# Gated delta rule recurrence: block-inverse joins as 32x32 and 64x64 products in tiles of the TensorE array

## The reference, cut to what matters

```python
lmat = jnp.where(strict, beta[..., :, None] * kk * decay, 0.0)
a = lmat + jnp.eye(CHUNK, dtype=lmat.dtype)
rhs = jnp.concatenate([v * beta[..., None], k * (beta * jnp.exp(g))[..., None]], axis=-1)
sol = lax.linalg.triangular_solve(a, rhs, left_side=True, lower=True, unit_diagonal=True)
...
def step(S, inp):
    v_new = u_c - jnp.einsum("bhcd,bhde->bhce", w_c, S)
    o_c = (jnp.einsum("bhcd,bhde->bhce", qd_c, S)
           + jnp.einsum("bhij,bhje->bhie", qk_c, v_new))
    S = S * gl_c[..., None, None] + jnp.einsum("bhcd,bhce->bhde", kd_c, v_new)
    return S, o_c
```

## Time and profile before

| what | value |
|---|---|
| time, median of 3 executions | 1723.73 us (1723.07 to 1731.12) |
| time of the profiled execution | 1730.97 us |
| its span on the core | 1729.2 us |
| PE busy | 1676.2 us, 97% of the span, 9103 matmul records |
| DVE, ACT, POOL busy | 49%, 40%, 50% |
| the recurrence | from 233.7 us to 507.1 us of the span |
| mean granted TensorE clock | 0.991 of full speed |

### The profile page before, as it was taken

The page is one execution under the profiler, slowest core; times in us unless marked ns, Lnnn a source line. Parts: engine busy times, 40 slices in busy tenths (PEclk is TensorE's granted clock), DMA queues, the critical chain, the costliest instruction groups (busy, mean ns, idle before and its releaser), DMA issues.

```text
span 1729.2 us, 22778 instructions
## 1 busy us (share of the span) xinstructions
PE 1676.2 (97%) x9103; PEld 1448.7 (84%) x9103; DVE 850.3 (49%) x1343; ACT 685.3 (40%) x1010; POOL 865.8 (50%) x485
## 2 busy tenths in 40 slices
PE   7999899999999999999999999999999999999997
PEld 7898889999989888888888887888887778888886
DVE  7778956824334201222111112127999974357754
ACT  5655444233232222234222223334233354366651
POOL 4455434233335544544555555446467466356661
PEclk9999899999999999999999999999999999999999
DMA  5476179454322324322322333333222322223332
GB/s 204 143 247 178 62 215 281 119 166 149 121 74 86 98 97 146 98 89 95 98 97 98 97 96 101 100 108 93 94 96 84 110 86 87 97 98 98 101 104 75
DMA packets 121264, 202.41 MB, mean 117 GB/s; under 512 B 32560, under 2 KB 71624, under 8 KB 121160
## 3 DMA queue, kind: packets, MB, share of 16 engines
q1 hardware_dynamic: 119400, 197.98, 36.1%
q10 hardware_dynamic: 1760, 2.98, 0.5%
HBM read 170.97 MB, written 29.97 MB: 116 GB/s over the span
## 4 chain that ended last, share of the span: by engine, by line
PE 80%; DVE 14%; ACT 2%; issue 2%; DMA 1%; SPq 0%; POOL 0%; DVEq 0%; ACTq 0%
PE ps L421 66%; DVE ps L1268 4%; PE ps L1775 4%; DVE cacc L2231 3%; PE ps L897 1%; PE ps L950 1%; PE ps L943 1%; PE ps L954 1%; PE ps L907 1%; PE ps L905 1%; DVE prd L632 1%; PE ps L929 1%; PE ps L937 1%; PE ps L915 1%; DVE inv L635 1%
## 5 line engine op out<-in xcount | busy, mean ns | idle before, releaser
L409 POOL TENSOR_TENSOR w_lo<-w_raw,w_hi 128x1024 fp32r<-128x1024 f32 x264 | 632.6, 2405 | 525.8 <-ACT w_hi L403 525.4
L421 PE MATMUL ps<-hp,w_hi 128*128 128x512 f32 (+2 forms) x2432 | 596.1, 345 | 4.8 <-DVE cacc L2231 3.2
L421 PEld LDWEIGHTS ps<-hp,w_hi 128*128 128x128 f32 x2432 | 405.2, 190 | 58.1 <-issue 4.3
L421 PE MATMUL ps<-hp,w_lo 128*128 128x512 f32 (+2 forms) x1216 | 371.5, 343 | 0.0
L403 ACT ACTIVATE w_hi<-w_raw 128x1024 fp32r<-128x1024 f32 x264 | 276.9, 1053 | 145.0 <-DMA w_raw<-in_w 137.3
L421 PEld LDWEIGHTS ps<-hp,w_lo 128*128 128x128 f32 x1216 | 212.2, 190 | 25.9
L421 PE MATMUL ps<-n_hi,w_hi 128*128 128x512 f32 x464 | 183.8, 396 | 2.1 <-POOL w_lo L409 2.1
L421 PE MATMUL ps<-n_hi,w_lo 128*128 128x512 f32 x464 | 180.7, 389 | 0.0
L421 PE MATMUL ps<-n_lo,w_hi 128*128 128x512 f32 x464 | 180.5, 389 | 0.0
L1268 DVE SCALAR_TENSOR_TENSOR ps<-u_in,par,ps 128x511 f32<-128x511 f32 (+14 forms) x240 | 176.7, 739 | 7.5
L421 PEld LDWEIGHTS ps<-n_hi,w_hi 128*128 128x128 f32 x464 | 87.1, 188 | 21.9 <-ACT sg_a L2065 2.5
(11 more groups left out here) (411 smaller groups left out, 2658.6 us busy)
## 6 DMA issues: line engine op xcount, KB each, us to landing
w_raw<-in_w SPq DMA_DIRECT2D x264, 512.0 KB, 3.4
d_y<-zero SPq DMA_DIRECT2D x6, 688.0 KB, 6.2
d_x<-zero SPq DMA_DIRECT2D x6, 688.0 KB, 6.0
d_at<-at SPq DMA_DIRECT2D x16, 256.0 KB, 3.1
d_kc<-kc SPq DMA_DIRECT2D x16, 256.0 KB, 3.2
d_qd<-eg SPq DMA_DIRECT2D x16, 256.0 KB, 3.2
d_p<-dec SPq DMA_DIRECT2D x16, 256.0 KB, 3.3
AT<-d_at SPq DMA_DIRECT2D x16, 256.0 KB, 6.2
```

Source lines behind the costliest of these rows:

```text
L409: e.tensor_tensor(w_lo[:, u % RAW, :], w_raw[:, u % RAW, :], w_hi[:, u % RAW, :].bitcast(F32), ALU.subtract).then_inc(s_lo, 1)
L421: mm = e.matmul(ov, w, r[:, k, t0:t1], start=(first and n == 0 and p3 == 0), stop=(last and n == len(tiles) - 1 and p3 == 2))
```

## The change: what it does

Every product of the joins is restricted to the blocks that are used. Both operands are sliced to 32 or 64 partitions (rows of the array) and 32 or 64 columns, and the output goes to 32 or 64 partitions of PSUM, so that each product takes one tile of the array. t32 becomes two 32x32 products for each head in place of one 128x128 product; yx four 32x32 products for each head in place of two that stream 64 columns; t64 and y64 one 64x64 product each. The copies of `act_tc` shrink from 128x512 elements to 128x128 at level 32 and 64x256 at level 64. The copies by `act_xc`, `dve_yc32` and `dve_yc64` keep their sizes and read other places of PSUM. Waits and the order of the groups stay.

```diff
         def half_cols(b, second):
-            return ps[:, b, 256 * second:256 * second + 256].rearrange("p (u n b) -> p u n b", u=HG, n=2)
+            return ps[:, b, 256 * second:256 * second + HG * BLK].rearrange("p (u b) -> p u b", u=HG)
+        def quad(n):
+            return slice(BLK * n, BLK * n + BLK)
+        def pairs32(s):
+            return [(2 * n + 1, 2 * n) if s == 0 else (2 * n, 2 * n + 1) for n in range(2)]
+        def sides(s):
+            return (slice(64, 128), slice(0, 64)) if s == 0 else (slice(0, 64), slice(64, 128))
...
             for u in range(HG):
-                mm = e.matmul(bankv(LB[s], P, P)[:, u], SQ[s]["AT"][:, u], SQ[s]["X"][:, u], start=True, stop=True)
+                if lev == 32:
+                    for i, j in pairs32(s):
+                        mm = e.matmul(half_cols(LB[s], 0)[quad(i), u], A[quad(j), u, quad(i)], X[quad(j), u, quad(j)], start=True, stop=True)
+                else:
+                    i, j = sides(s)
+                    mm = e.matmul(bankv(LB[s], P, 64)[i, u], A[j, u, i], X[j, u, j], start=True, stop=True)
...
             for u in range(HG):
-                e.matmul(half_cols(LB[s], 0)[:, u], T[:, u], blocks(Y, 1 - s)[:, u], start=True, stop=True)
-            for u in range(HG):
-                mm = e.matmul(half_cols(LB[s], 1)[:, u], Y[:, u], blocks(T, s)[:, u], start=True, stop=True)
+                for i, j in pairs32(s):
+                    r = quad(i)
+                    e.matmul(half_cols(LB[s], 0)[quad(j), u], T[r, u, 0:BLK], Y[r, u, r], start=True, stop=True)
+                    mm = e.matmul(half_cols(LB[s], 1)[r, u], Y[r, u, r], T[r, u, 0:BLK], start=True, stop=True)
...
             for u in range(HG):
-                mm = e.matmul(bankv(LB[s], P, 64)[:, u], T[:, u], Y[:, u, c], start=True, stop=True)
+                mm = e.matmul(bankv(LB[s], P, 64)[j, u], T[i, u, 0:64], Y[i, u, i], start=True, stop=True)
...
-            e.activation(SQ[s]["TR"][:], bankv(LB[s], P, P), ACT.Copy).then_inc(q_tc[s].sem, 1)
+            if lev == 32:
+                e.activation(SQ[s]["TR"][:, :, 0:BLK], half_cols(LB[s], 0), ACT.Copy).then_inc(q_tc[s].sem, 1)
+            else:
+                i, _ = sides(s)
+                e.activation(SQ[s]["TR"][i, :, 0:64], bankv(LB[s], P, 64)[i], ACT.Copy).then_inc(q_tc[s].sem, 1)
```

More of the change, by code:

```diff
@@ L895, in pe_t @@
                 e.wait_ge(*q_yc[s].at(2 * k))
+            A, X = SQ[s]["AT"], SQ[s]["X"]
             for u in range(HG):
-                mm = e.matmul(bankv(LB[s], P, P)[:, u], SQ[s]["AT"][:, u], SQ[s]["X"][:, u], start=True, stop=True)
+                if lev == 32:
[4 more added lines that the diff above has]
+                    mm = e.matmul(bankv(LB[s], P, 64)[i, u], A[j, u, i], X[j, u, j], start=True, stop=True)
             mm.then_inc(q_t[s].sem, 1)
         def pe_yx(e, s, k):
-            T, X, Y = SQ[s]["TR"], SQ[s]["X"], SQ[s]["Y"]
+            T, Y = SQ[s]["TR"], SQ[s]["Y"]
             e.wait_ge(s_ld["Y"][s], 16 * (k + 1))
@@ L912, in pe_y64 @@
             e.wait_ge(*q_tc[s].at(2 * k + 1))
-            c = slice(0, 64) if s else slice(64, 128)
+            i, j = sides(s)
             for u in range(HG):
-                mm = e.matmul(bankv(LB[s], P, 64)[:, u], T[:, u], Y[:, u, c], start=True, stop=True)
+                mm = e.matmul(bankv(LB[s], P, 64)[j, u], T[i, u, 0:64], Y[i, u, i], start=True, stop=True)
             mm.then_inc(q_y64[s].sem, 1)
@@ L964, in act_tc @@
                 e.wait_ge(*q_yx[s].at(k))
-            e.activation(SQ[s]["TR"][:], bankv(LB[s], P, P), ACT.Copy).then_inc(q_tc[s].sem, 1)
+            if lev == 32:
[3 more added lines that the diff above has]
+                e.activation(SQ[s]["TR"][i, :, 0:64], bankv(LB[s], P, 64)[i], ACT.Copy).then_inc(q_tc[s].sem, 1)
         def act_xc(e, s, k):
             e.wait_ge(*q_yx[s].at(k))
[L969 to L972, removed]
+            for i, j in pairs32(s):
+                m = e.activation(SQ[s]["X"][quad(i), :, quad(j)], half_cols(LB[s], 1)[quad(i)], ACT.Copy, scale=-1.0)
             m.then_inc(q_xc[s].sem, 1)
@@ L988, in dve_yc32 @@
             e.wait_ge(*q_yx[s].at(k))
[L989 to L992, removed]
+            for i, j in pairs32(s):
+                m = e.tensor_scalar(SQ[s]["Y"][quad(j), :, quad(i)], half_cols(LB[s], 0)[quad(j)], -1.0, None, ALU.mult)
             m.then_inc(q_yc[s].sem, 1)
@@ L996, in dve_yc64 @@
             e.wait_ge(*q_y64[s].at(k))
-            r, c = (slice(64, 128), slice(0, 64)) if s else (slice(0, 64), slice(64, 128))
-            e.tensor_scalar(SQ[s]["Y"][r, :, c], bankv(LB[s], P, 64)[r], -1.0, None, ALU.mult).then_inc(q_yc[s].sem, 1)
+            i, j = sides(s)
+            e.tensor_scalar(SQ[s]["Y"][j, :, i], bankv(LB[s], P, 64)[j], -1.0, None, ALU.mult).then_inc(q_yc[s].sem, 1)
         def dve_r(e, s, k):
```

2 lines of the change are left out of this document (removed).

## The result

The changed kernel takes 1705.64 us (median of 5 runs, 1704.65 to 1714.26) where the kernel before took 1723.73 (5 runs, 1723.07 to 1731.12): ratio 0.9897, with a 95% interval of 0.9877 to 0.9918. It is faster, by 18 us or 1.0%; 1705 was predicted. The profiled span is 1712.5 us against 1729.2, 16.7 us less.

The account below looks back on a forecast made before the run. PE's issue time was taken to bound the kernel nearly everywhere. Gains of 22.3 us less 3.4 for clock falls gave 18.9, taken off 1723.7, the profiled 1730.97 less 7 for the median: 1705 us, range 1694 to 1725.

Parts of the forecast that it names:

- steps 4 and 5: Recurrence steps where DVE is busy throughout: only 0.3 us passed on, where PE would give 3.7.
- steps 6 to 14: Nine steady recurrence steps, each 1.83 us shorter with tiles side by side: 16.5 us.
- The price of the narrow groups: Joins in a steady step: gains of 0.57 us for y64 with t32, 1.17 for yx, 0.09 for t64.
- the series price: yx's 32 narrow records one after another, 0.026 us apart: 0.83 us, against 0.21 over four tiles.
- The price of changing shape: Edges of narrow groups on PE: into 64 columns 0.15 us, into 32 0.13, back to whole array 0.20.
- The clock: PE's new idle time in steps 0 to 2 and 4 to 5: two falls to half clock charged, 3.4 us.
- The loop of DVE, DMA and DVE: Steps 0 to 2: this loop doesn't shorten, so steps 1 and 2 give only 0.9 us each.
- Series: Rival for t32 and yx: tiles don't overlap, records run one after another; 1712 us, chance 0.27.
- Every change of tile: Rival within t32 and yx: each change of tile costs like a change of shape; slower, 1740 us, chance 0.07.
- Row groups: Rival within t32 and yx: only changes of the row group cost, 0.10 us each; 1728 us, chance 0.11.
- Twice the record: Rival for t32 and yx: a narrow record costs 0.052 us, twice the row's; about 1722 us, chance 0.02.
- The gain into waits: Rival: DVE and DMAs bound more steps, or the clock falls five times or more; 1713 to 1722 us, chance 0.11.

Follow-up runs that it names:

- e3: The change with the four heads of one tile issued in a row, so that neighbouring records share a tile: 1709.89 us, ratio 0.9929.
- e11: The change with t32 and yx narrowed in columns only, their operands keeping all 128 rows of the array: 1703.49 us, ratio 0.9875.
- e8: e4 plus the sums for sc_v ahead of VN and the substitution recut, with less ahead of VN in step 5: 1701.42 us, ratio 0.9872.
- c1: The changed kernel itself, unedited, measured and profiled again: 1705.10 us, ratio 0.9891.
- c2: The changed kernel itself, unedited, measured once more, beside e11 and on its chip: 1706.13 us, ratio 0.9891.
- e4: The change with DVE's write of Y for t64 moved ahead of one part of the substitution in steps 4 and 5: 1702.53 us, ratio 0.9887.
- e9: e8 with DVE's write of Y placed between the two halves of the gate preparation in steps 0 to 2: 1699.40 us, ratio 0.9872.
- c3: The kernel of e9 measured once more, beside the change: 1701.83 us, ratio 0.9869.

## Why the prediction was right

By its terms, in us (measured from one profile of each kernel, first ks to first ks):

| term | predicted | measured |
|---|---|---|
| ahead of step 0 | 1.85 | 1.2 |
| steps 0 to 2, with the clock | 1.9 - 3.4 | 0.1 |
| step 3 | 1.5 | 1.1 |
| steps 4 and 5 | 0.3 | 0.05 |
| steps 6 to 14 | 16.5 | 14.3 |
| step 15 | 0.24 | 0.1 |
| sum | 18.9 | 16.8 |

**The price of the narrow groups: right.** In a steady step, t64 with its edges gave 0.09 us (0.09 predicted), y64 with t32 0.60 (0.57), yx 1.17 to 1.21 (1.17). The last: yx itself went from 1.71 to 0.38 us, w ahead of it from 0.89 to 0.98, and the units behind it are 0.02 to 0.06 longer. Six of the nine steps from 6 to 14 gained 1.86 to 1.93 us; predicted was 1.83. Tiles side by side, taken from the four column tiles of L1136, were the right choice: the 32 records of yx start within 0.26 us, where the series price was 0.83. The prediction's 0.21 us for both t32 and yx is eight records of the fullest tile at 0.026 us each, and the starts show just this; only the distance is 0.032 us in a tile of 32 columns, where L776 with 16 has 0.025 to 0.026. That e3's yx comes to 0.83 us doesn't confirm the series price: 0.12 of it is the way to the next group, and its tiles still overlap in part. The 0.056 us for a 64-column record was 0.058.

**The price of changing shape: right.** Into a narrow shape the last distance is 0.205 us for 0.112, so 0.09 (0.10 predicted); then the distance behind the first record is longer by another 0.05 for 64 columns (0.05 predicted) and 0.02 for 32 (0.03). Back to the whole array from t64 it is 0.09 and 0.10 (0.20 together).

The Trainium skill, "TensorEngine Tiling (Array Packing)", section Key Properties, has a drain at a change of mode and none at a change of tile. The trace agrees: 0.205 us at the first, 5 to 12 ns at the second. The Trainium skill, "TensorEngine Tiling (Array Packing)", section Restrictions and Gotchas, says that row tiles can't use one PSUM bank at once. Neighbours in yx start 5 to 12 ns apart into one bank, and e11, without row tiles, takes the same time: the rule shows no cost here.

**Steps 6 to 14: the mis-sized term.** The step "nine times 1.83" left out that the shorter yx uncovers DVE work queued behind VN in steps 10 and 12. They gained 0.75 us each, step 14 1.41 (a wait of 0.40 for VN). The words "in steps 6 to 14 DVE, ACT and POOL are each busy a third of the time" argued from an average, and the average said nothing about the order on DVE. e8 shows the cause: with that order turned round, both steps take 1.11 us less.

**Up to step 5: near in sum, by errors that cancel.** The terms from ahead of step 0 to step 5 come to 2.15 us predicted and 2.4 measured, but their parts were off both ways.

- *The clock.* Two falls were charged, and the profile after has two, at 237.5 and 258.0 us. The number is luck: c1 and c2 have other ones, a longer stretch over the start of step 0 and, in c2, one in step 3. The fall at 503.4 us, at the end of step 15 before, is there after the change too, at 486.7. The price was near: step 1, with a fall, took 13.59 us in the profile after, and 11.66 in seven others without one (c1, c2, e4, e8, e9, c3, e11); so a fall costs 1.9 us there (1.7 charged). The one at 237.5 began ahead of step 0 and slowed t64 there from 0.61 to 1.03 us, a part of why that stretch gave 1.2 and not 1.85.
- *The loop of DVE, DMA and DVE.* It was said not to shorten, and steps 1 and 2 to give 0.9 us each. Without a fall and without the next wait, step 1 took 11.66 us for 13.20 and step 2 11.6 to 12.0 for 13.06: 1.0 to 1.5 us each. So the prediction put this gain too low. Which part of the loop became shorter, the runs don't tell.
- *A wait that it didn't have.* PE waits 1.2 to 1.5 us at L532 for ACT's eg, in step 0 of the profile after, in step 2 of c1, e8 and e11, in none of c2's for more than 0.3. At w it waited 0.9 to 1.3 us in steps 0 to 2, where 2 and more was forecast.
- *Step 3* gave 1.1 of 1.5: the wait at w grew from 0.46 to 1.34 us and took what y64 and t32 had brought.
- *Steps 4 and 5.* The loss was to stand at t64, nearly 2 us each. It was 1.79 at t32 in step 4, and 0.35 for VN and 1.16 at t64 in step 5; in c2 it was 1.3 and 1.2 at t64. That DVE bounds these steps is shown by e4 and e8: the order on DVE alone gives 1.2 to 2.1 and 2.0 to 3.0 us there.

**The rivals.** Series: no, by the starts of yx, and by e3 against the change. Every change of tile: no, by the distances of 5 to 12 ns. Row groups: no, by e11. Twice the record: no, by 0.032 us. The gain into waits: part of it, 2.2 us in steps 10 and 12 and most of steps 4 and 5, too little to decide.

**The step to the median, and luck.** The sum was made on the profiled 1730.97 us and came to 1712.1; the profiled execution after took 1714.3 (its span is 1712.5), so the sum was 2.2 us too good there. Taking 7 us off for the median fitted, because the profiles of both kernels happened to catch the longer stretch ahead of the recurrence that is told of below; nothing made sure of that. The medians are 18.1 us apart, the profiles 16.7, and no term explains the rest. So 1705 for 1705.64 is nearer than the terms are: they carry an error of about 2 us.

**A better version.** e9 and e8 stand at ratios of 0.9872 where the change beside them has 0.9891; the intervals overlap. Their profiles show the 2.2 us in steps 10 and 12 and the 2 to 3 in steps 4 and 5 as gained, about 0.2 to 0.3% of the kernel.

## What to carry to other kernels

Small products in fp32 were paid here by their columns and not by their rows: narrow the columns, place neighbouring products in different column tiles, let the product index change fastest over tiles so that every tile has the same short list of records, and put narrow groups next to each other, since leaving the whole array and coming back costs about 0.3 us (yx costs 0.50 to 0.53 us with its edges, 0.26 of it the 32 records; t64 0.80, 0.46 of it the records). Before you count a shorter group on the bounding engine as gained in every step, read for each kind of step what the other engines do during it, in their order: work that was hidden behind it may now end last. A busy share of a third doesn't answer that.

## What the runs showed of the hardware that was not expected

**Tiles overtake each other in the records.** Ahead of step 0 the records of L840, whose four products stand wholly ahead of yx in the program, mix with those of yx. From the PE timeline of the profile after:

```profile
234.69 0.19 PE L920 MATMUL ps<-Y,TR 32*32 32x32 f32 x1
234.72 0.27 PE L840 MATMUL ps<-v_met,m_dec 16*16 16x128 f32 x1
234.72 0.19 PE L920 MATMUL ps<-Y,TR 32*32 32x32 f32 x1
```

So the order of starts of a trace is not program order where products lie in different tiles. The yx of e3 shows the same.

**DVE held by POOL.** In three profiles (before, after, e4), 62 operations of the substitution each, 11 in all take over 1.2 us between 285 and 337 us; each of them began up to 0.7 us behind a start of L409 on POOL and ended 0.2 to 0.3 us behind its end. The Trainium skill, "GPSIMD Engine Reference", section Specifications, says that POOL shares its SBUF interfaces with VectorE, with contention for DVE instructions with two SBUF inputs. The rows agree; they add the size: 2.46 us for 0.4, as long as POOL's operation lasts.

**A stretch ahead of the recurrence that differs by 6 to 10 us from one execution to another.** The profiles of before and after reach the first t32 at 233.7 and 233.8 us, all the others at 224 to 227.3, though the programs are the same up to there. PE's waits from 150 us to there, in the profile after and then in c1:

```profile
PE ps L722 <- ACT vT L1853: 6.0, 3, 2.4
PE ps L421 <- DVE cacc L2245: 3.2, 2, 2.8
```

```profile
PE ps L421 <- DVE cacc L2245: 2.8, 1, 2.8
```

Six of the us are three waits for ACT, which c1 has not. The granted clock differs there too: at 0.50 from 193.2 to 196.6 and from 210.2 to 217.0 us in the profile after, from 159.1 to 165.9 in c1. The two profiled executions took 1730.97 and 1714.26 us in all, the other runs of these kernels about 1723 and 1705. What decides between them wasn't tried. A difference of under 10 us between two profiled spans has to be looked for first ahead of the recurrence.
